# The v projection of a gated-linear-attention block as seven block products instead of sixteen full matmuls

## What is computed

```python
h = rmsnorm(x)
proj = h @ w_in                      # columns: u_h | gate_b | gate_c | q | k | v | g | gk_low
y_conv = gate_b * causal_depthwise_conv3(gate_c * u_h)
o = gla_chunked(q * dk**-0.5, k, v, log_a)        # 4 heads, dk 64, dv 128, chunks of 64
y_gla = rmsnorm(o) * silu(g_out)
x = x + concatenate([y_conv, y_gla]) @ w_out
x = x + moe(rmsnorm(x))              # 32 experts, top 4, clamped SwiGLU
out = rmsnorm_final(x)
```

## Time and profile before

| | us |
|---|---|
| median of 3 runs | 1022.93 (1022.27 to 1023.39) |
| the profiled execution's own time | 1022.09 |
| its span, first to last instruction | 1020.3 |
| TensorE busy | 998.4 (98% of the span) |
| VectorE busy | 279.9 (27%) |
| ScalarE busy | 149.9 (15%) |
| GpSimd busy | 10.8 (1%) |

### The profile page before, as it was taken

One profiled execution on the slowest core, in us unless ns is written; L12 is line 12 of the kernel. 1 busy time (PEld: TensorE's weight loads), 2 busy tenths in 40 slices (PEclk: granted clock), 3 DMA queues, 4 the chain that ended last, 5 costly groups with the idle time before them and its releaser, 6 DMA issues.

```text
span 1020.3 us, 12891 instructions
## 1 busy us (share of the span) xinstructions
PE 998.4 (98%) x5032; PEld 413.1 (40%) x5032; DVE 279.9 (27%) x685; ACT 149.9 (15%) x302; POOL 10.8 (1%) x29
## 2 busy tenths in 40 slices
PE   9999999999999999999999999999999999999997
PEld 7799733333333333333333333333333333333334
DVE  2888522222212221222221222212221221122122
ACT  2311311111111111111111111111111111111112
POOL 1010000000000000000000000000000000000000
PEclk9999999999999999999999999999999999999999
DMA  9986999999999999999999999999999999999996
GB/s 371 424 337 252 405 380 416 430 432 433 427 429 430 432 432 430 430 432 430 430 432 432 432 432 432 432 432 432 432 432 430 432 432 432 430 426 430 426 422 259
DMA packets 24662, 423.87 MB, mean 415 GB/s; under 512 B 3000, under 2 KB 3648, under 8 KB 7360
## 3 DMA queue, kind: packets, MB, share of 16 engines
q1 hardware_dynamic: 23616, 422.10, 97.3%
q10 hardware_dynamic: 1024, 1.47, 0.4%
HBM read 422.51 MB, written 1.05 MB: 415 GB/s over the span
## 4 chain that ended last, share of the span: by engine, by line
PE 80%; DMA 18%; SPq 1%; issue 1%; DVE 0%; ACT 0%; POOL 0%; ACTq 0%; PEldq 0%; DVEq 0%; POOLq 0%
PE bank L1867 33%; PE bank L1888 18%; DMA ring<-in_w_expert 14%; PE bank L1517 5%; PE bank L1726 4%; PE y L1931 4%; DMA ring<-in_w_down_last 4%; PE bank L1906 3%; PE y L1667 2%; PE bank L1802 1%; PE bank L1570 1%; PE bank L1509 1%; PE bank L1985 1%; PE bank L1912 1%; PE bank L1667 1%; SPq L599 1%
## 5 line engine op out<-in xcount | busy, mean ns | idle before, releaser
L1867 PE MATMUL bank<-ring,x_t 128*64 128x512 f32 x1984 | 447.3, 597 | 0.2 <-DVE x_t L1330 0.2
L1867 PEld LDWEIGHTS bank<-ring,x_t 128*64 128x64 f32 x1984 | 134.1, 136 | 262.8 <-issue 259.3
L1888 PE MATMUL bank<-ring,act 128*64 128x512 f32 x960 | 223.0, 596 | 7.4 <-DMA ring<-in_w_expert 7.4
L1370 DVE TENSOR_TENSOR gu_b<-bank,bias_t 128x512 f32<-128x512 f32 x64 | 44.3, 692 | 323.5 <-PE bank L1906 323.4
L1888 PEld LDWEIGHTS bank<-ring,act 128*64 128x64 f32 x960 | 66.3, 137 | 133.5 <-issue 133.5
L836 ACT COPY gu_sb<-bank 128x512 f32<-128x512 f32 x64 | 37.5, 586 | 222.7 <-PE bank L1867 222.7
L1323 DVE TENSOR_TENSOR x_t<-bank,cols 128x512 f32<-128x512 f32 x30 | 20.7, 691 | 165.1 <-PE bank L1802 165.1
L1931 PE MATMUL y<-z,p_t 64*128 64x512 f32 x240 | 59.6, 615 | 0.0
L1726 PE MATMUL bank<-x_sb,p_row 128*64 128x512 f32 x248 | 58.5, 592 | 0.0
L1309 DVE TENSOR_SCALAR p_row<-slot,rank,rstd 128x64 f32<-128x64 f32 x62 | 16.6, 312 | 147.6 <-PE bank L1912 147.6
L840 ACT ACTIVATE act<-gu_b 128x256 f32<-128x256 f32 x62 | 25.8, 417 | 192.1 <-DVE gu_b L1376 192.1
(11 more groups left out here) (275 smaller groups left out, 537.7 us busy)
## 6 DMA issues: line engine op xcount, KB each, us to landing
ring<-in_w_expert SPq DMA_DIRECT2D x72, 4096.0 KB, 30.7
ring<-in_w_expert SPq DMA_DIRECT2D x34, 2048.0 KB, 15.1
ring<-in_w_expert SPq DMA_DIRECT2D x14, 1024.0 KB, 8.7
ring<-in_w_in SPq DMA_DIRECT2D x4, 2048.0 KB, 25.7
ring<-in_w_down_last SPq DMA_DIRECT2D x6, 1024.0 KB, 40.9
ring<-in_w_out SPq DMA_DIRECT2D x2, 2048.0 KB, 26.8
ring<-in_w_expert SPq DMA_DIRECT2D x8, 512.0 KB, 5.0
ring<-in_w_in SPq DMA_DIRECT2D x2, 1024.0 KB, 12.5
```

The source lines that it names most:

```text
L1370: dve.tensor_tensor(gu_b[:, :, :, :], bank[2][:, :].rearrange("p (f a s) -> p a f s", a=2, f=4), bias_t[:, :, 4 * h:4 * h + 4, ds(e, 1)] . ...
L1867: ins = mm(bank[h][a * SLOTS:(a + 1) * SLOTS, :], x_t_of(it)[:, k, :], w[:, kk, a, :], start=k == 0, stop=k == KT - 1)
L1888: ins = mm(bank[0][a * SLOTS:(a + 1) * SLOTS, :], act_of(it)[:, k, :], w[:, kk, a, :], start=k == 0, stop=k == KT - 1)
```

## The change

v's projection uses the scheme of `project_blocked` with the roles swapped: the activation block is stationary and 256 columns of weight move. TensorE:

```diff
+            def multiply_v(acc, h, w, first, last):
+                for k in range(4):
+                    ins = mm(acc, h[:, k, :], w[:, k, :], start=first and k == 0, stop=last and k == 3, skip_group_check=True)
+                ins.then_inc(s_pj, 1)
...
-            project_v(0, range(2))
+            pe.wait_ge(s_v0, 16)
+            multiply_v(v_a, h_block(0, 0), v_block(0, 0), True, False)
             pe.wait_ge(s_pkd, 1)
...
-            project_v(0, range(2, KT))
-            project_v(1, range(KT))
+            pe.wait_ge(s_slot[mix_slot(VV)], 16)
+            multiply_v(v_b, h_block(1, 0), v_block(0, 1), True, True)
+            pe.wait_ge(s_ts, 5)
+            pe.wait_ge(s_gkb, 1)
+            multiply_v(v_d, x_sums[:, 1, :, :], v_diff, True, False)
+            pe.wait_ge(s_sum, 1)
+            pe.wait_ge(s_bck, 1)
+            multiply_v(v_c, x_sums[:, 0, :, :], v_sum, True, False)
+            pe.wait_ge(s_ts, 6)
+            pe.wait_ge(s_pk, 1)
+            multiply_v(v_a, x_sums[:, 2, :, :], v_less, False, True)
+            pe.wait_ge(s_pk, 2)
+            multiply_v(v_d, x_sums[:, 3, :, :], v_block(1, 1), False, True)
+            pe.wait_ge(s_ts, 7)
+            pe.wait_ge(s_pk, 3)
+            multiply_v(v_c, h_block(1, 1), v_block(0, 1), False, True)
...
+            pe.wait_ge(s_pk, 4 + TT)
```

The last line stands behind block 0, before the outer products that read `v_row`. GpSimd, after its constants:

```diff
+            pool.wait_ge(s_v0, 16)
+            pool.wait_ge(s_slot[mix_slot(VV)], 16)
+            pool.tensor_tensor(v_sum[:, :, :], v_block(1, 0), v_block(1, 1), ALU.add).then_inc(s_sum, 1)
+            pool.wait_ge(s_ss, 1)
+            pool.tensor_tensor(v_both[:, :, :], v_block(0, 0), v_block(0, 1), ALU.add).then_inc(s_sum, 1)
```

ScalarE keeps four products, and scales v by rstd when all four quadrants (`s_diag` at TT + QUADS = 6) are there; `keep_parts(0)` follows, unchanged:

```diff
-            keep_v(3)
+            keep_v_part(0, 1, v_a)
+            keep_v_part(2, 4, v_d)
+            keep_v_part(1, 3, v_c)
...
-            keep_v(4)
+            keep_v_part(3, 5, v_a)
+            act_e.wait_ge(s_diag, TT + QUADS)
+            for t in range(TT):
+                act_e.activation(v_row[:, t, :], v_row[:, t, :], ACT.Copy, scale=rstd[:, t:t + 1]).then_inc(s_pk, 1)
```

VectorE makes the activation sums right after h (four of them, the last two each from the one before), `v_diff` after the rstd diagonals, two more weight sums behind the gate's bias, and the quadrants of v among the sums of block 0:

```diff
+            dve.wait_ge(s_h, KT)
+            dve.tensor_tensor(x_sums[:, 0, :, :], h_block(0, 1), h_block(0, 0), ALU.subtract).then_inc(s_ts, 1)
...
+            dve.tensor_tensor(v_diff[:, :, :], v_block(0, 0), v_block(1, 0), ALU.subtract).then_inc(s_ts, 1)
...
+            dve.wait_ge(s_sum, 1)
+            dve.tensor_tensor(v_less[:, :, :], v_sum[:, :, :], v_block(0, 0), ALU.subtract).then_inc(s_ts, 1)
+            dve.wait_ge(s_sum, 2)
+            dve.wait_ge(s_pj, V_PRODUCTS[2])
+            dve.tensor_tensor(v_block(0, 1), v_both[:, :, :], v_sum[:, :, :], ALU.subtract).then_inc(s_ts, 1)
...
             scale_h(0)
+            scale_h(1)
             sum_1(0)
-            sum_3(0)
-            scale_h(1)
             dve.wait_ge(s_hs, 2)
             dve.tensor_tensor(h_sums[:, 0, :, :], ...)
+            dve.wait_ge(s_pk, 1)
+            dve.tensor_tensor(v_rows(0, 0), v_b, v_parts[:, 0, :], ALU.add).then_inc(s_diag, 1)
             dve.tensor_tensor(h_sums[:, 1, :, :], ...)
+            sum_3(0)
+            dve.wait_ge(s_ts, 8)
+            dve.tensor_tensor(h_sums[:, 2, :, :], ...)
             sum_2(0)
-            dve.wait_ge(s_ts, 1)
-            dve.tensor_tensor(h_sums[:, 2, :, :], ...)
-            dve.wait_ge(s_ts, 3)
+            dve.wait_ge(s_ts, 10)
             dve.tensor_tensor(h_sums[:, 3, :, :], ...)
+            dve.wait_ge(s_pk, 4)
+            link(dve.tensor_tensor(v_parts[:, 1, :], v_parts[:, 1, :], v_parts[:, 2, :], ALU.add))
+            dve.tensor_tensor(v_rows(1, 1), v_parts[:, 3, :], v_parts[:, 1, :], ALU.add).then_inc(s_diag, 1)
             sum_4(0)
+            dve.tensor_tensor(v_rows(1, 0), v_d, v_parts[:, 3, :], ALU.add).then_inc(s_diag, 1)
+            dve.tensor_tensor(v_rows(0, 1), v_c, v_parts[:, 3, :], ALU.add).then_inc(s_diag, 1)
```

More of the change, by code:

```diff
@@ L52 @@
 PRODUCTS, SUMS, PARTS, QUADS = 7, 4, 4, 4
+V_SUMS = 2
 FIRST, SECOND = PRODUCTS * len(BLOCKED), PRODUCTS * (len(BLOCKED) + 1)
@@ L265, in build @@
         o_sq = y_t[:, 0:CT, :]
-        junk = at("junk", [P, D], slot_at(9))
+        junk = at("junk", [P, 2, D], slot_at(9))
+        v_diff = at("v_diff", [P, 4, 2 * P], slot_at(9) + 4096)
+        v_less = at("v_less", [P, 4, 2 * P], slot_at(9) + 8192)
+        v_both = at("v_both", [P, 4, 2 * P], slot_at(9))
+        v_parts = at("v_parts", [P, PARTS, 2 * P], slot_at(9) + 12288)
+        x_sums = at("x_sums", [P, 4, 4, P], 8192)
+        v_sum = at("v_sum", [P, 4, 2 * P], 16384)
         diag = at("diag", [P, TT, P], slot_at(9) + 2 * 4096)
@@ L332, in build @@
         s_pj = sem("projected")
-        s_pk = sem("v_kept")
+        s_pk = sem("v_parts_and_rows_kept")
         s_pkd = sem("projection_scaled")
-        s_diag = sem("rstd_diagonal_ready")
+        s_diag = sem("rstd_diagonals_and_v_quadrants_ready")
         s_bc = sem("rstd_spread")
@@ L428, in build @@
         s_pool = sem("pool_step")
-        PROJ = [(QK, 0), (QK, 1), ("gk", 0), (VV, 0), (VV, 1)]
+        PROJ = [(QK, 0), (QK, 1), ("gk", 0)]
+        V_PRODUCTS = {product: len(PROJ) + 1 + i for i, product in enumerate((1, 2, 4, 3, 5, 6, 7))}
         TURN_BANK = ((0, 3), (5, 6))
@@ L442, in w_block, with v_block, v_rows @@
             return chunk_view(BLOCKED[c], KT)[:, 4 * half:4 * half + 4, 2 * P * m:2 * P * (m + 1)]
+        def v_block(m, half):
+            return chunk_view(VV, KT)[:, 4 * half:4 * half + 4, 2 * P * m:2 * P * (m + 1)]
+        def v_rows(m, t):
+            return v_row[:, t, 2 * P * m:2 * P * (m + 1)]
         def h_block(half, t):
@@ L459, in build @@
         out_a, out_b, out_c, out_d = ([bank[i][:, 0:2 * P] for i in banks] for banks in ((5, 1), (6, 4), (7, 7), (4, 2)))
+        v_a, v_b, v_c, v_d = (bank[i][:, 0:2 * P] for i in (3, 6, 7, 4))
         acc_a, acc_b, acc_c, acc_d = (bank[i][:, 0:2 * P].rearrange("p (a t) -> p a t", a=2) for i in (1, 2, 3, 0))
@@ L488, in _ @@
                 if c >= MIX_SLOTS:
-                    sp.wait_ge(s_pj, PROJ.index((c - MIX_SLOTS, 1)) + 1)
+                    sp.wait_ge(s_pj, PROJ.index((QK, 1)) + 1 if c == MIX_SLOTS else V_PRODUCTS[7])
                 src = w_in[c - 1] if c < WO else w_out[c - WO]
@@ L716, in _ @@
             act_e.wait_ge(s_x[0], 16)
-            square_sum(0, junk[:, :])
+            square_sum(0, junk[:, 0, :])
             act_e.wait_ge(s_x[1], 16)
-            square_sum(1, y_t[:, 0:4, :].rearrange("p k t -> p (k t)"))
+            square_sum(1, junk[:, 1, :])
             for t in range(TT):
@@ L725, in _, with keep_v_part @@
             act_e.dma_start(br_bc[:, :], b_router.partition_broadcast(P)[:, 0, :]).then_inc(s_late, 16)
[L727 to L730, removed]
+            def keep_v_part(p, product, src):
+                act_e.wait_ge(s_pj, V_PRODUCTS[product])
+                act_e.copy(v_parts[:, p, :], src).then_inc(s_pk, 1)
             act_e.wait_ge(s_gkb, 1)
@@ L961, in _ @@
                     dve.tensor_scalar(h_t[:, k, :], h_t[:, k, :], g_mix[:, k:k + 1], None, ALU.mult).then_inc(s_h, 1)
+            dve.wait_ge(s_h, KT)
+            dve.tensor_tensor(x_sums[:, 0, :, :], h_block(0, 1), h_block(0, 0), ALU.subtract).then_inc(s_ts, 1)
+            dve.tensor_tensor(x_sums[:, 1, :, :], h_block(1, 1), h_block(0, 1), ALU.subtract).then_inc(s_ts, 1)
+            dve.wait_ge(s_ts, 1)
+            dve.tensor_tensor(x_sums[:, 2, :, :], h_block(1, 1), x_sums[:, 0, :, :], ALU.subtract).then_inc(s_ts, 1)
+            dve.wait_ge(s_ts, 3)
+            dve.tensor_tensor(x_sums[:, 3, :, :], h_block(1, 0), x_sums[:, 2, :, :], ALU.subtract).then_inc(s_ts, 1)
             dve.wait_ge(s_cols, 16)
@@ L967, in _ @@
                 dve.tensor_scalar(diag[:, t, :], ident[:, :], rstd[:, t:t + 1], None, ALU.mult).then_inc(s_diag, 1)
+            dve.wait_ge(s_v0, 16)
+            dve.tensor_tensor(v_diff[:, :, :], v_block(0, 0), v_block(1, 0), ALU.subtract).then_inc(s_ts, 1)
             dve.wait_ge(s_bc, 1)
@@ L984, in scale_h @@
             def scale_h(t):
-                dve.wait_ge(s_pj, PROJ.index((VV, t)) + 1)
+                dve.wait_ge(s_pj, V_PRODUCTS[(2, 7)[t]])
                 c = slice(t * P, (t + 1) * P)
@@ L1001, in sum_2 @@
             def sum_2(c):
-                dve.wait_ge(s_sum, SUMS * c + 1)
+                dve.wait_ge(s_sum, V_SUMS + SUMS * c + 2)
                 dve.wait_ge(s_prod, PRODUCTS * c + 1)
@@ L1007, in sum_4 @@
             def sum_4(c):
-                dve.wait_ge(s_sum, SUMS * c + 3)
+                dve.wait_ge(s_sum, V_SUMS + SUMS * c + 3)
                 dve.wait_ge(s_prod, PRODUCTS * c + 2)
@@ L1071, in _ @@
             scale_h(0)
+            scale_h(1)
             sum_1(0)
-            sum_3(0)
-            scale_h(1)
             dve.wait_ge(s_hs, 2)
             dve.tensor_tensor(h_sums[:, 0, :, :], h_block(0, 1), h_block(0, 0), ALU.subtract).then_inc(s_ts, 1)
+            dve.wait_ge(s_pk, 1)
```

(26 more changed lines are left out.)

## The result

The changed kernel takes 1028.2 us (median of 4 runs, 1027.66 to 1028.5); the kernel before takes 1022.6 beside it (1021.54 to 1023.39). That is +5.6 us, ratio 1.0056 with a 95% interval of 1.0043 to 1.0068: slower. The profiled execution took 1028.5 us and its span is 1026.7, 6.4 longer than before.

The account below looks back on a forecast made before the run. TensorE bounds the mixer and the expert-weight stream the end, with no slack between. A 4.4 us stall less 1.67 us of v's gain leaves +2.9: 1022.93 + 2.9 = 1025.8 us, range 1024.6 to 1028.6.

Parts of the forecast that it names:

- the case without the lower clock: TensorE's stall before block 0's fifth product eats v's 1.67 us; +2.9, 1025.8 us, chance 0.52.
- the first rival: The clock falls in TensorE's stall before block 0's fifth product: +4.7, 1027.6 us, chance 0.22.
- Bound and stream: TensorE's gain or loss before about 127 us moves the expert-weight stream and the end by as much.
- TensorE's work: In v, 32 instructions (13.74 us) give way to 56 narrower ones (12.07 us): 1.67 us gained if nothing waits.
- Activation sums and `v_diff` at no cost: On VectorE, four sums (2.6 us) fit a 3.52 us wait and `v_diff` (1.14 us) ends before the next input: cost 0.
- GpSimd's sums: Two weight additions at 2.15 us each, ending at 22.2 and 24.35 us; slow-GpSimd rival 3.3 us each, +5.2, chance 0.07.
- The exclusion of 0.8 us: VectorE's `v_less` stands until GpSimd's `v_both` ends at 24.35 us, so the gate's chain starts 0.8 us later.
- VectorE's list: From `scale_h(1)` to v's fourth quadrant 9.97 us, ready at 43.4; rival of a shorter list: 1024.6 us, chance 0.12.
- ScalarE: After v's last quadrant it scales two rows and copies the first part before TensorE goes on at 45.05 us.
- The idle: TensorE stalls 4.4 us before block 0's fifth product, from 40.6 to 45.05 us.
- The clock: After TensorE's stall in block 0, a relapse to the lower level costs 1.8 us, or 5.4 over all three products.
- the other side's 1021.3: ScalarE's wait for the quadrants is met before about 39.2 us, so 1.67 us are gained: 1021.3, chance 0.04.

Follow-up runs that it names:

- the filled experiment: 16 unused matmuls of 128 columns put in front of TensorE's wait for ScalarE's first copy, against the changed kernel; 1025.79 us, ratio 1.0032 to the kernel before.

## Why the prediction was right or wrong

The direction, the place and the mechanism of the stall were right, and 1028.2 lies in the range of 1024.6 to 1028.6, but near its end: the forecast of +2.9 (1025.8) was the case without the lower clock, and the case that came was the first rival (+4.7, 1027.6, given 0.22) against +5.6 measured. The forecast's own number was met by no run of this kernel; the range held because the rival was in it.

- **Bound and stream: right.** +6.5 us at the end of block 0 are +6.4 at the end of the span. In all twelve profiles, of kernels whose block 1 begins anywhere from 49.1 to 56.4 us, the rest of the span behind that point takes 969.9 to 970.9 us.
- **TensorE's work: right.** 0.2155 us an instruction was forecast; eight take 1.73, 0.216 each. The gain of 1.67 was 1.63.
- **Activation sums and `v_diff` at no cost: right.** They ran from 11.40 to 14.39 us and VectorE's next input came at 14.91. The last of the four took 1.06 instead of 0.69 beside GpSimd's selections, so half a microsecond of cover was left.
- **GpSimd's sums: 2.15 us forecast, 2.36 measured;** started at 19.93 where 20.0 was taken:

```profile
19.93 2.35 POOL L686 TENSOR_TENSOR v_sum<-ring 128x1024 f32<-128x1024 f32 x1 [3.80 <-DMA ring<-in_w_in]
22.24 2.36 POOL L688 TENSOR_TENSOR v_both<-ring 128x1024 f32<-128x1024 f32 x1
```

  The first began 0.2 us after v's weights had landed and took as long as the second, so no start cost of 6 us lay in it or before it, here or in any other profile with these sums. The Trainium skill (GPSIMD Engine Reference, Instruction dispatch) states that cost for the first call of a freshly loaded routine; whether this routine counts as one, no run shows.
- **The exclusion of 0.8 us: right, but not in every execution.** In the profiled one `v_less` started at 24.68, just after `v_both` had ended at 24.60, since the start was 1.14 us late; in the filled experiment and with the second sum put back `v_less` took 2.01 and 2.57 us. Between two versions that differ only in that sum the price is 0.8 to 0.9 us.
- **VectorE's list: right.** 9.97 us forecast from `scale_h(1)` to the last quadrant; 34.24 to 44.20 is 9.96.
- **ScalarE: right.** From the last quadrant to TensorE 1.65 forecast, 1.73 measured.
- **The idle: 4.4 forecast, 4.14 measured.** The difference is mostly the exclusion that this execution escaped.
- **The clock: the step that failed.** I let it stay up in the likeliest case, because no row had so long an idle, and priced a fall by the warm-up's length, 1.8 us (5.4 if it lasted over all three products). It fell in the profiled execution and cost 2.88 us (2.64 against the 5.60 us of the filled experiment). The term of the sum that was missing is this one: 4.14 + 2.88 - 1.63 makes +5.4; without the fall it would be +2.5, close to the forecast's +2.9. The stretches show why the price was low: the level was already down before TensorE resumed, and stayed down for about 5.5 us of work where the warm-up had 3.35. The Trainium skill (TensorE: Matmul & The Clock Gate, Why this matters for your kernels) states that a long enough idle between bursts brings the lower level. The traces agree for the idle of 4.14 us (0.50), and one of 2.5 us had no fall in the one profile that has it (1.00); but the last section has a fall behind a shorter one. In the warm-up the granted clock reads 1.00 though instructions took twice their time; later in the span that column did show the fall.
- **What I left out.** With the stall gone v's gain still did not show, because VectorE's list was also full behind block 0: another 1.0 us. I had checked the waits inside block 0 and taken those behind it as unchanged relative to TensorE, which held only while the stall gave VectorE time. It did not touch this forecast, but it did touch the other side's 1021.3: with ScalarE's wait out of the way the time was 1022.52.

What stays open: the runs without the second sum and with the state wait spread over 3.4 us, and all three profiles of that kernel are of executions under 1022 us. Whether its long executions have a lower clock there was not seen; their mean granted clock of 0.997 against 0.998 is a smaller step than the 0.995 of the executions with the long fall.

## What to carry to other kernels

A wait that is put into an in-order engine's program belongs to everything queued behind it: ask who needs the next instruction, not who needs this one. Here a scaling whose result TensorE reads only behind block 0, three products and 5.4 us later, stood in front of a copy that TensorE needed at once, and moving it gave back 5.4 of 5.6 us. Then follow the freed engine to the next full list: the saving of 1.5 us arrived only when two more places on VectorE had been cleared. And cost an idle of TensorE of 4 us, as here, as the idle plus a possible stretch at half clock behind it (2.9 us here); filling it with unused matmuls kept the clock up in the one kernel that tried it, when the wait itself stayed.

## What the runs showed of the hardware that I had not expected

- An idle of 4.14 us was followed by the lower clock in both profiles that have it, and perhaps not in every execution: five runs of one kernel stand at 1026.0 to 1026.2 and at 1028.1 to 1029.2 us. In both profiles the level fell while TensorE still stood, 2.9 us after its last matmul in one (at about 44.6 us) and 2.3 us after it in the other (43.7).
- The length of the idle alone does not decide. In the changed kernel's own profile the level fell a second time, at about 812.6 us, 1.2 us after TensorE had resumed from a wait of 1.99 us for expert weights, and stayed at 0.50 for some 3.4 us. It cost nothing that the end of the span shows. The waits of 1.8 us for such weights in the kernel before were followed by no fall, nor was the one of 2.5 us above.
- The start of a kernel is not constant either: the same 64 instructions take 14.0 to 15.2 us from profile to profile, which is as much as this change can gain. The difference between the changed kernel and the one before lies ahead of 8 us: 15 instructions began or ran in the two stretches from 4 to 8 us instead of 20, and from 8 us on both have 11 in two microseconds. The rest of the span behind block 0 scatters by 1.0 us as well (969.9 to 970.9), and neither explains the 3.4 and 3.6 us over which the runs of two versions spread.
- The second half of v's weights was issued at 6.2 to 6.5 us in nine of the twelve profiles and had landed by 20.0. In the other three it was issued at 6.9, 7.0 and 7.1 us and landed at 20.5, 21.7 and 22.1: half a microsecond of issue can become two of landing. In the last, GpSimd's first sum began at 22.27 instead of 19.93, and with both sums TensorE lost 2.0 us by the two waits behind it; with the landing at 21.7, in a profile without the second sum, it lost under 0.1 us.
